# Two heads side by side, on the two halves of the array's columns, in a decoder step's prompt attention

## The chip, the cores and the metric
The kernel runs on one core of one Trainium2 chip. The metric is the device time of one execution in microseconds: 1531.83 us is the median of three runs (1531.2 to 1532.99).

## The reference
One inference step of a two-layer decoder (model width 1024) for a prompt of 512 tokens and eight sample sequences of one token each, all in float32. Layer 0 has a dilated sliding-window softmax attention with 8 heads of 64 (called A here) beside a gated linear attention with 4 heads. Layer 1 (called C) has 16 query heads on 4 key heads; an indexer picks 128 keys for each query, and only these take part. Each layer ends with a SwiGLU FFN and a gated per-layer input. For a query block, attention is

```python
s = jnp.einsum('btngd,btknd->btkng', qg, kg).reshape(bx, t, k, h).astype(jnp.float32) + bias
s = jnp.where(valid[..., None], s, -jnp.inf)
lse = jax.nn.logsumexp(s, axis=2)
p = jnp.exp(s - lse[:, :, None, :]).reshape(bx, t, k, n_kv, grp)
o = jnp.einsum('btkng,btknd->btngd', p.astype(vg.dtype), vg).reshape(bx, t, h, d)
```

The kernel computes C with a mask over all earlier keys in place of a gather, and A with the dilations folded into the bias table.

## The kernel before
Activations lie with features on the 128 partitions and the 520 tokens (512 of the prompt, 8 samples) along the free axis. Every weight matrix is a stream of blocks of 128x1024. SyncE loads a block, ScalarE rounds it (`w_hi`, L1396), POOL takes the rest (`w_lo`, L516), and TensorE multiplies three times (hi by hi, hi by lo, lo by hi; `block_products`, L750). TensorE's queue is one written order: input projection, prompt attention, output projection, FFN, gate, for layer 0 and then layer 1. Engines wait for each other by counting semaphores.

Prompt attention (`attention` on each engine) is a list of units. A unit is a pair `p` of heads, one head `par` of the pair, and a query block `qb` of 128 queries; it covers 128 x (qb + 1) keys. There are 4 pairs in A (32 units) and 8 in C (64 units), and the order is pair, head, query block. A unit goes through these steps:
- `scores` (TensorE, L848 and L851): in C a matmul adds the mask, then two matmuls with the high and low parts of the queries, into one of two score banks.
- `add_bias` (VectorE, L1921): adds the bias from PSUM and takes the maximum.
- `exps` (ScalarE, L1483), then `scale` (VectorE, L1927 and L1929): exponentials and their sum, then division by it.
- `turn` (TensorE, L860): a transpose for each key block. `copy` (ScalarE, L1490) brings the result back into one of two buffers `pt`.
- `out` (TensorE, L872): for each key block a matmul with values as weights. Values of a head are padded with zeros to 128 columns (`vA`, `vC`), so both heads of a pair add into the same bank: 128 partitions, of which the head's own 64 get values and the others zeros.

TensorE's iteration i does scores of unit i, the transposes of unit i-3, the output of unit i-4, and then what `sample_a` or `sample_c` puts in at that i: the samples' attention (L1159 and L1171 in A, whose weights have 64 columns; L1314 and L1331 in C), norms and transposes. When a pair's eight units are done, ScalarE (L1494) and VectorE (L1934) split its result for the output projection.

Before a stage starts, heads are staged: POOL makes high, repeated and low parts of a query head (L612 and L618 in A, `place_q_part` at L700 to L704 in C), ScalarE and VectorE do the same for keys (L1684 and L2162 in A; L1833 and L2306 in C), and POOL zeroes the padding and places the values. In C, VectorE first finds the 128 largest index scores of each query (L2287 and L2291) and makes the masks (L2312).

In the first layer `values_by_token` (L1002) is a group of matmuls whose weights have 64 columns and which go in turns to partitions 0 to 63 and 64 to 127 of one bank; `sample_updates` (L1077) has eight records on one half and then eight on the other.

## Time and profile before

| what | value |
|---|---|
| median of three runs | 1531.83 us (1531.2 to 1532.99) |
| the profiled execution's own time | 1531.57 us |
| its span in the profile | 1529.8 us |
| mean granted TensorE clock | 0.991 |
| TensorE busy | 1496.5 us, 98% |
| VectorE, ScalarE, POOL busy | 623.9, 652.2, 761.6 us |
| first scores of attention A, of attention C | at 199.59 us, at 922.80 us |
| first output-projection matmul after C | at 1038.96 us |

The engines are named PE (TensorE matmuls), PEld (its weight loads), DVE (VectorE), ACT (ScalarE), POOL and SP (SyncE). "L872" is line 872 of the kernel. A float32 matmul leaves two records in the trace, so counts of records are twice the counts of such matmuls in the code. Matmul records overlap: the step from one start to the next tells the rate, and the duration of one does not. Instructions of one kind that follow each other are merged in the timeline, with their count and the time from the first start to the last end.

### The profile page before, as it was taken

Reading aid. Unit: us, or ns where it says so; the run is one execution under the profiler, and the core shown is the slowest. Engines: PE = TensorE matmul, PEld = TensorE weight load, DVE = VectorE, ACT = ScalarE, POOL = GpSimd, SP = SyncE. Lnnn points to the kernel's source line nnn. Section 1 sums busy time; section 2 is a strip of 40 time slices with the busy share of each in tenths; the row PEclk is TensorE's granted clock in tenths of the full one; section 3 lists DMA queues with packets and bytes.
Section 4 is the critical chain, followed back from the end, with each engine's and each line's share of the span. In section 5 each row is a group of like instructions: output and inputs, shape, how many; then the busy total and the mean of one; then the engine's idle time right before and its main releaser. Section 6 shows DMA issues by size and latency. Waiting matters only on the chain.

```text
span 1529.8 us, 30921 instructions
## 1 busy us (share of the span) xinstructions
PE 1496.5 (98%) x12032; PEld 1428.4 (93%) x12032; DVE 623.9 (41%) x1176; ACT 652.2 (43%) x1095; POOL 761.6 (50%) x589
## 2 busy tenths in 40 slices
PE   7999998999999999999999997999999999999998
PEld 6999976699999999999999786999999999999998
DVE  4035556335333333212361796873433233222224
ACT  5242555325344344222464556663443444432234
POOL 4655674064554554555436476324454554554543
PEclk9999989999999999999999998999999999999999
DMA  5321433223233223333234231132222232223332
GB/s 175 91 98 57 152 135 107 70 96 98 83 95 96 84 95 96 97 96 100 93 94 122 90 94 63 54 86 70 83 96 89 92 94 91 89 95 99 107 96 98
DMA packets 52980, 145.84 MB, mean 95 GB/s; under 512 B 5501, under 2 KB 18329, under 8 KB 52394
## 3 DMA queue, kind: packets, MB, share of 16 engines
q1 hardware_dynamic: 50490, 136.12, 28.4%
q10 hardware_dynamic: 2416, 8.72, 1.6%
q8 instruction: 48, 0.79, 0.2%
q14 instruction: 26, 0.21, 0.0%
HBM read 138.06 MB, written 6.76 MB: 95 GB/s over the span
## 4 chain that ended last, share of the span: by engine, by line
PE 91%; DVE 4%; ACT 2%; issue 1%; DMA 1%; POOL 1%; SPq 0%; ACTq 0%; DVEq 0%; POOLq 0%
PE PS L750 74%; PE PS L872 3%; PE PS L965 2%; PE PS L851 2%; PE PS L860 1%; PE PS L788 1%; PE PS L1159 1%; PE PS L1171 1%; DMA w_raw<-in_w 1%; PE PS L1244 1%; PE PS L848 1%; PE PS L1314 1%; DVE act_lo L1901 0%; DVE sqsum L1892 0%; PE PS L1331 0%
## 5 line engine op out<-in xcount | busy, mean ns | idle before, releaser
L516 POOL TENSOR_TENSOR w_lo<-w_raw,w_hi 128x512 fp32r<-128x512 f32 x428 | 594.4, 1409 | 688.1 <-ACT w_hi L1396 680.6
L750 PE MATMUL PS<-act_hi,w_hi 128*128 128x260 f32 x2464 | 701.6, 285 | 0.8 <-DVE act_lo L2178 0.7
L750 PE MATMUL PS<-act_lo,w_hi 128*128 128x260 f32 x2464 | 695.4, 282 | 0.0
L750 PE MATMUL PS<-act_hi,w_lo 128*128 128x260 f32 x2464 | 694.9, 282 | 0.0
L1396 ACT ACTIVATE w_hi<-w_raw 128x1024 fp32r<-128x1024 f32 x214 | 226.9, 1060 | 685.5 <-PE PS L750 665.9
L750 PEld LDWEIGHTS PS<-act_hi,w_hi 128*128 128x128 f32 x2464 | 463.5, 188 | 15.0 <-issue 12.3
L750 PEld LDWEIGHTS PS<-act_lo,w_hi 128*128 128x128 f32 x2464 | 463.8, 188 | 0.4
L750 PEld LDWEIGHTS PS<-act_hi,w_lo 128*128 128x128 f32 x2464 | 464.0, 188 | 0.0
L750 PE MATMUL PS<-h_hi,w_lo 128*128 128x260 f32 x704 | 198.8, 282 | 0.0
L750 PE MATMUL PS<-h_hi,w_hi 128*128 128x260 f32 x704 | 198.6, 282 | 0.0
L750 PE MATMUL PS<-h_lo,w_hi 128*128 128x260 f32 x704 | 198.5, 282 | 0.0
L750 PEld LDWEIGHTS PS<-h_hi,w_hi 128*128 128x128 f32 x704 | 132.6, 188 | 0.0
L750 PEld LDWEIGHTS PS<-h_lo,w_hi 128*128 128x128 f32 x704 | 132.3, 188 | 0.0
L750 PEld LDWEIGHTS PS<-h_hi,w_lo 128*128 128x128 f32 x704 | 132.2, 188 | 0.0
L1981 DVE TENSOR_TENSOR x<-PS,x 128x520 f32<-128x520 f32 x16 | 11.2, 700 | 178.7 <-PE PS L750 178.7
L1966 DVE TENSOR_TENSOR tmp<-PS,nrs 128x520 f32<-128x520 f32 x44 | 30.8, 699 | 110.9 <-PE PS L750 101.2
L1968 DVE TENSOR_TENSOR tmp<-PS,sq 128x520 f32<-128x520 f32 x44 | 30.8, 699 | 103.7 <-ACT sq L1537 103.7
L1892 DVE TENSOR_TENSOR sqsum<-sqsum,sq 128x520 f32<-128x520 f32 x48 | 63.9, 1332 | 21.2 <-ACT sq L1402 20.4
L1972 DVE TENSOR_TENSOR tmp<-PS,tmp 128x520 f32<-128x520 f32 x44 | 30.8, 700 | 94.5 <-PE PS L750 94.5
L1490 ACT ACTIVATE tmp<-PS 128x128 f32<-128x128 f32 (+1 forms) x96 | 41.4, 431 | 59.2 <-PE PS L860 59.2
L1901 DVE SCALAR_TENSOR_TENSOR act_lo<-x,vecs,act_hi 128x520 fp32r<-128x520 f32 x48 | 48.7, 1031 | 21.8 <-ACT act_hi L1407 21.7
L1976 DVE TENSOR_TENSOR h_lo<-tmp,h_hi 128x520 f32 x44 | 34.9, 794 | 40.2 <-ACT h_hi L1541 40.2
(350 smaller groups left out, 1903.7 us busy)
## 6 DMA issues: line engine op xcount, KB each, us to landing
w_raw<-in_w SPq DMA_DIRECT2D x214, 512.0 KB, 3.5
kcA<-in_cache_k SPq DMA_DIRECT2D x8, 512.0 KB, 4.7
biasC<-scratch_rows SPq DMA_DIRECT2D x12, 256.0 KB
vcA<-in_cache_v SPq DMA_DIRECT2D x4, 512.0 KB, 5.2
kcC<-in_pool_k SPq DMA_DIRECT2D x16, 128.0 KB, 2.6
vcC<-in_pool_v SPq DMA_DIRECT2D x16, 128.0 KB, 2.2
out_y<-x SPq DMA_DIRECT2D x7, 260.0 KB, 4.3
x<-in_xT SPq DMA_DIRECT2D x3, 520.0 KB, 6.7
```

What stands on the lines that cost most here:

```text
L516: ins = pool.tensor_tensor(w_lo[:, s, cols], w_raw[:, s, cols], w_hi[:, s, cols].bitcast(F32), ALU.subtract)
L750: mm = pe.matmul(PS[:, 2 * place + half, 0:HALF], w[:, s, j * P:(j + 1) * P], r[:, c, cols], start=first and n == 0 and i == 0, stop=last ...
L851: mm = pe.matmul(PS[:, score_bank(base, i), 0:W], q_of[part][par][:, p % 2, qb * P:(qb + 1) * P], k[:, k_chunk(p), 0:W], start=part == 0 a ...
L872: mm = pe.matmul(PS[:, 4 + p % 2, qb * P:(qb + 1) * P], v_of(p, par, kb), pt[:, i % 2, kb * P:(kb + 1) * P], start=i % 8 == 0, stop=i % 8 ...
L1396: act.activation(w_hi[:, s, :], w_raw[:, s, :], ACT.Copy).then_inc(S("w_hi"), 1)
L1490: act.activation(pt[:, i % 2, 0:W], PS[:, turned_bank(base, i), 0:W], ACT.Copy).then_inc(S("t_c"), 1)
L1892: dve.tensor_tensor(sqsum[:], sqsum[:], sq[:, m % 2, :], ALU.add).then_inc(S("ssum"), 1)
L1901: dve.scalar_tensor_tensor(act_lo[:, c, :], x[:, c, :], vecs[:, g:g + 1], act_hi[:, c, :].bitcast(F32), ALU.mult, ALU.subtract).then_inc(S ...
L1966: dve.tensor_tensor(halves(tmp[:, 1, :]), slot(0), halves(nrs[:]), ALU.mult).then_inc(S("f_a"), 1)
L1968: dve.tensor_tensor(halves(tmp[:, 1, :]), slot(0), halves(sq[:, 0, :]), ALU.mult).then_inc(S("free_v"), 1)
L1972: dve.tensor_tensor(halves(tmp[:, 0, :]), slot(1), halves(tmp[:, 1, :]), ALU.mult).then_inc(S("free_v"), 1)
L1976: dve.tensor_tensor(h_lo[:, bass.ds(f, 1), :], tmp[:, 0:1, :], h_hi[:, bass.ds(f, 1), :].bitcast(F32), ALU.subtract).then_inc(S("h_lo"), 1)
```

## The change
- Units are ordered pair, query block, head: both heads of a pair side by side.
- `out` does two units at once, on odd iterations (units i-5 and i-4). Its matmuls alternate between the heads. Each has a head's 64 value columns as weights and writes that head's 64 partitions. The padded values, their zeroing and their placing are gone.
- `pt` has four buffers; the two new ones are the ones that held padded values (`rs`), which are also the head norm's, hence the wait for the last norm in `copy`.
- In C the keys of the first and second half of the pairs ("T") are staged apart: the first before the stage, the second at iterations 14, 15 (ScalarE) and 18, 19 (VectorE). The third mask is made after the first unit's bias. The head norm before the last moves behind the first exponentials. Query staging starts a block earlier.
- The samples' queries in C are placed by two copies for each half of the heads, in place of two for each pair.
- POOL's long element-wise instructions are done in two halves.
- Bias rows of a later pair are asked for when the last unit of the same head two pairs before has its bias added.

```diff
-        pt = tmp[:, :, 0:SEQ]
+        pt = (tmp[:, 0, 0:SEQ], tmp[:, 1, 0:SEQ], rs[:, 0, 0:SEQ], rs[:, 1, 0:SEQ])
...
         def units_of(pairs):
 
-            return [(p, par, qb) for p in range(pairs) for par in range(2) for qb in range(QB)]
+            return [(p, par, qb) for p in range(pairs) for qb in range(QB) for par in range(2)]
...
             def bias_a(p, par):
 
-                sp.wait_ge(S("t_x"), BASE_A + 8 * (p - 2) + 4 * par + 6)
+                sp.wait_ge(S("t_x"), BASE_A + 8 * (p - 2) + par + 9)
...
+            def in_halves(out, t, u, op):
+
+                n = out.shape[-1] // 2
+                for half in range(2):
+                    at = (slice(None),) * (len(out.shape) - 1) + (slice(n * half, n * half + n),)
+                    ins = pool.tensor_tensor(out[at], t[at], u[at], op)
+                return ins
+
             def low(b, s):
 
                 pool.wait_ge(S("w_hi"), b + 1)
-                for half in range(2):
-                    cols = slice(DM // 2 * half, DM // 2 * half + DM // 2)
-                    ins = pool.tensor_tensor(w_lo[:, s, cols], w_raw[:, s, cols], w_hi[:, s, cols].bitcast(F32),
-                                             ALU.subtract)
-                ins.then_inc(S("w_lo"), 1)
+                in_halves(w_lo[:, s, :], w_raw[:, s, :], w_hi[:, s, :].bitcast(F32),
+                          ALU.subtract).then_inc(S("w_lo"), 1)
...
-            def zero_v(par):
-                pool.memset(vA[par][:, :, :, other[par]], 0.0).then_inc(S("A_zero"), 1)
...
-            def place_v(pair, par):
...
             def first_q_c(n):
-                if n == 14:
+                if n == 13:
                     pool.wait_ge(S("i_r"), 24)
                     pool.wait_ge(S("d_z"), 3)
-                    pool.memset(vC[0][:, :, :, other[0]], 0.0).then_inc(S("C_zero"), 1)
-                if 14 <= n < 18:
+                if 13 <= n < 17:
                     pool.wait_ge(S("hn_ok"), n + 2)
-                    for k in ((0, 1), (2,), (3, 4), (5,))[n - 14]:
+                    for k in ((0, 1), (2,), (3, 4), (5,))[n - 13]:
                         place_q_part(0, k)
 
             products_in(1, first_q_c)
 
-            pool.wait_ge(S("hn_ok"), 19 + 2)
-            pool.memset(vC[1][:, :, :, other[1]], 0.0).then_inc(S("C_zero"), 1)
-            pool.wait_ge(S("C_zero"), 2)
             for p in range(1, PAIRS_C):
...
                 def out(i):
-                    p, par, qb = units[i]
-                    if par == 0 and qb == 0:
+                    p, _, qb = units[i]
+                    if qb == 0:
                         pe.wait_ge(S("t_o"), base // 8 + p + 1)
-                    pe.wait_ge(S("t_c"), base + i + 3)
-                    if qb == 0 and valued is not None:
-                        valued(p, par)
+                    if p == 0:
+                        valued(qb)
+                    pe.wait_ge(S("t_c"), base + i + 4)
                     for kb in range(qb + 1):
-                        mm = pe.matmul(PS[:, 4 + p % 2, qb * P:(qb + 1) * P], v_of(p, par, kb),
-                                       pt[:, i % 2, kb * P:(kb + 1) * P], start=i % 8 == 0,
-                                       stop=i % 8 == 7 and kb == qb)
-                    mm.then_inc(S("t_v"), 1)
+                        for par in range(2):
+                            mm = pe.matmul(PS[HD * par:HD * par + HD, 4 + p % 2, qb * P:(qb + 1) * P], v_of(p, par, kb),
+                                           pt[(i + par) % 4][:, kb * P:(kb + 1) * P], start=qb == 0,
+                                           stop=qb == QB - 1 and kb == qb)
+                    mm.then_inc(S("t_v"), 2)
...
-                        out(i - 4)
+                    if i >= 5 and i % 2:
+                        out(i - 5)
...
-            def values_staged_a(p, par):
-                if p == 0 and par == 0:
-                    pe.wait_ge(S("hn_ln"), 8 + 1)
-                pe.wait_ge(S("A_zero"), par + 1)
-                pe.wait_ge(S("A_st"), 4 * p + 3 + par)
+            def values_staged_a(qb):
+                pe.wait_ge(S("hn_ln"), 8 + 1)
+                pe.wait_ge(S("A_v"), qb + 1)
...
                 def copy(i):
                     W = P * (units[i][2] + 1)
                     act.wait_ge(S("t_t"), base + i + 3)
-                    act.wait_ge(S("t_v"), base + i + 1)
-                    act.activation(pt[:, i % 2, 0:W], PS[:, turned_bank(base, i), 0:W], ACT.Copy).then_inc(S("t_c"), 1)
+                    act.wait_ge(S("t_v"), base + (max(i - 2, 0) // 2) * 2)
+                    if i == 2:
+                        act.wait_ge(S("hn_ok"), (19 if base else 8) + 2)
+                    act.activation(pt[i % 4][:, 0:W], PS[:, turned_bank(base, i), 0:W], ACT.Copy).then_inc(S("t_c"), 1)
...
-                    if q is not None:
+                    if q is not None and not (final and l == 1):
...
-            def sample_q(t):
-                act.wait_ge(S("hn_ok"), 11 + t + 1 + 2)
+            def sample_q(T):
+                act.wait_ge(S("hn_ok"), 11 + 4 * T + 4 + 2)
                 for r in range(2):
                     rows = slice(HD * r, HD * r + HD)
-                    cols = qzC[rows, t // 4 * NS:(t // 4 + 1) * NS, :].rearrange("p b c -> p (b c)")
-                    c0 = 64 * r + NS * t
-                    act.activation(cols[:, c0:c0 + 7 * 129 + 1:129], yC[rows, 10 + t, SEQ:NT],
+                    by_token = qzC_flat[rows, NS * P * T:NS * P * T + NS * (P + 1)].rearrange("p (b c) -> p b c", c=P + 1)
+                    c0 = 64 * r + 4 * NS * T
+                    act.activation(by_token[:, :, c0:c0 + 3 * NS + 1:NS],
+                                   yC[rows, 10 + 4 * T:14 + 4 * T, SEQ:NT].rearrange("p t b -> p b t"),
                                    ACT.Copy).then_inc(S("C_st8"), 1)
 
-            def values_c(par):
+            def values_c():
 
                 for n in range(2):
                     act.wait_ge(S("v_vt"), n + 5)
-                    by_head = PS[:, 6 + n, :].rearrange("p (k t d) -> p t k d", k=2, t=2)
-                    act.activation(vC[par][:, :, 2 * n:2 * n + 2, HD * par:HD * par + HD],
-                                   by_head[:, :, :, HD * par:HD * par + HD], ACT.Copy).then_inc(S("C_st8"), 1)
+                    act.activation(vtokC[:, :, 2 * n * P:(2 * n + 2) * P].rearrange("p t (k d) -> p t k d", d=P),
+                                   PS[:, 6 + n, :].rearrange("p (k t d) -> p t k d", k=2, t=2),
+                                   ACT.Copy).then_inc(S("C_st8"), 1)
 
             def first_staging_c(n):
 
                 if n == C_BLOCKS - 1:
-                    values_c(0)
-                    act.wait_ge(S("act_free"), 4 + KC - 1 + 2)
-                    for k, rows in ((act_hi, slice(0, HD)), (act_lo, slice(HD, P))):
-                        act.activation(k[rows, 3:8:4, 0:SEQ], yC[rows, 6:8, 0:SEQ], ACT.Copy).then_inc(S("k_hi"), 1)
+                    act.wait_ge(S("act_free"), 4 + KC - 1 + 1)
+                    high_keys(0, 0)
+                    high_keys(1, 0)
+                    values_c()
+
+            def high_keys(par, T):
+                rows = slice(HD * par, HD * par + HD)
+                act.activation((act_hi, act_lo)[par][rows, 3 + 4 * T, 0:SEQ], yC[rows, 6 + T, 0:SEQ],
+                               ACT.Copy).then_inc(S("k_hi"), 1)
 
             last_head_rms_c, last_high_c = products_in(1, indexer, first_staging_c)
             def sample_c(i):
 
-                if i == 3:
+                if i == 0:
+                    last_head_rms_c(1)
+                elif i == 3:
                     last_head_rms_c()
                 elif i == 4:
                     last_high_c()
-                elif i == 5:
-                    act.wait_ge(S("hn_ok"), 19 + 2)
-                    values_c(1)
                 elif i in (6, 7):
...
+                elif i in (14, 15):
+                    if i == 14:
+                        act.wait_ge(S("act_free"), 4 + KC - 1 + 2)
+                    high_keys(i - 14, 1)
...
-            def low_keys(par):
+            def low_keys(par, T):
                 k = (act_hi, act_lo)[par]
                 rows, others = slice(HD * par, HD * par + HD), slice(HD - HD * par, P - HD * par)
-                dve.wait_ge(S("k_hi"), 3 + par)
-                dve.tensor_tensor(k[others, 3:8:4, 0:SEQ], yC[rows, 6:8, 0:SEQ], k[rows, 3:8:4, 0:SEQ].bitcast(F32),
-                                  ALU.subtract).then_inc(S("k_split"), 1)
-
-            low_keys(0)
-            for qb in range(1, QB):
+                dve.wait_ge(S("k_hi"), 3 + 2 * T + par)
+                dve.tensor_tensor(k[others, 3 + 4 * T, 0:SEQ], yC[rows, 6 + T, 0:SEQ],
+                                  k[rows, 3 + 4 * T, 0:SEQ].bitcast(F32), ALU.subtract).then_inc(S("k_split"), 1)
+
+            def mask(qb):
                 W = P * (qb + 1)
                 dve.tensor_scalar(maskC[:, qb, 0:W], work[qb][:, 0:W], GONE, NEG, ALU.not_equal,
                                   ALU.mult).then_inc(S("topk"), 1)
-            low_keys(1)
-            dve.wait_ge(S("topk"), QB)
+
+            low_keys(0, 0)
+            mask(1)
+            low_keys(1, 0)
+            mask(2)
+            dve.wait_ge(S("topk"), QB - 1)
...
-                if i == 6:
+                if i == 0:
+                    mask(3)
+                    dve.wait_ge(S("topk"), QB)
+                elif i in (18, 19):
+                    low_keys(i - 18, 1)
```

## Rows read from the trace of the kernel before

**Rows 1.** The page, part 1: busy us (share of the span) xinstructions.
```profile
PE 1496.5 (98%) x12032; PEld 1428.4 (93%) x12032; DVE 623.9 (41%) x1176; ACT 652.2 (43%) x1095; POOL 761.6 (50%) x589
```

**Rows 2.** The page, part 4: chain that ended last, by engine.
```profile
PE 91%; DVE 4%; ACT 2%; issue 1%; DMA 1%; POOL 1%; SPq 0%; ACTq 0%; DVEq 0%; POOLq 0%
```

**Rows 3.** Groups by line, L872: count | busy us, mean ns | idle before.
```profile
L872 PE MATMUL PS<-tmp,rs 128*128 128x128 f32 x240 | 35.4, 278 | 0.7 <-ACT tmp L1490 0.7
...
L872 PE MATMUL PS<-tmp,vtokC 128*128 128x128 f32 x160 | 23.6, 278 | 2.0 <-issue 1.6 <-ACT tmp L1490 0.2
...
L872 PE MATMUL PS<-tmp,vstA 128*128 128x128 f32 x80 | 12.7, 292 | 0.1
```

**Rows 4.** Timeline of PE, attention C: start us, us, what, [idle before].
```profile
967.51 0.33 PE L851 MATMUL PS<-act_lo,q_hiC 128*128 128x128 f32 x1
...
969.92 0.60 PE L860 MATMUL PS<-const,pC 128*128 128x128 f32 x4
...
970.94 0.48 PE L848 MATMUL PS<-maskC,identR 128*128 128x512 f32 x1
971.26 0.40 PE L851 MATMUL PS<-act_lo,q_hiC 128*128 128x512 f32 x1
...
971.84 1.06 PE L872 MATMUL PS<-tmp,vtokC 128*128 128x128 f32 x8
...
972.65 0.31 PE L851 MATMUL PS<-act_hi,q_hiC 128*128 128x128 f32 x1
```

**Rows 5.** Windows: stretch, length, busy us (count) by engine, PEclk, DMA, GB/s.
```profile
975.00:1000.00 25.00, 24.81 (x197) 22.96 (x196) 22.11 (x78) 17.33 (x54) 11.81 (x15) 1.00 0.18 57
1000.00:1035.00 35.00, 34.13 (x270) 31.91 (x270) 25.14 (x95) 22.58 (x68) 5.79 (x7) 1.00 0.27 81
920.00:930.00 10.00, 5.42 (x29) 4.60 (x28) 8.43 (x12) 5.18 (x10) 6.54 (x5) 0.80 0.01 2
```

**Rows 6.** Timeline of PE around L1002, column halves in turns.
```profile
88.52 0.28 PE L750 MATMUL PS<-act_hi,w_lo 128*128 128x260 f32 x1
88.73 1.97 PE L1002 MATMUL PS<-const,yA 128*64 128x128 f32 x32
90.63 0.39 PE L750 MATMUL PS<-act_hi,w_hi 128*128 128x260 f32 x1
90.86 0.28 PE L750 MATMUL PS<-act_lo,w_hi 128*128 128x260 f32 x1
```

**Rows 7.** Timeline of PE, L1077: eight on one half, then eight.
```profile
166.29 1.58 PE L1077 MATMUL PS<-vt,kz 8*64 8x128 f32 x16
```

**Rows 8.** Timeline of PE, attention A: L872 ahead of 64-column L1159.
```profile
237.13 0.39 PE L872 MATMUL PS<-tmp,vstA 128*128 128x128 f32 x2
...
237.45 1.95 PE L1159 MATMUL PS<-kcA,yA 128*64 128x257 f32 x8
```

**Rows 9.** Timeline at the entry of attention C: VectorE, then PE.
```profile
920.83 1.76 DVE L2306 TENSOR_TENSOR act_hi<-yC,act_hi 64x1024 fp32r<-64x1024 f32 x1 [1.61 <-ACT act_hi L1833]
...
925.59 2.19 DVE L2306 TENSOR_TENSOR act_lo<-yC,act_lo 64x1024 fp32r<-64x1024 f32 x1
...
927.81 0.29 DVE L1921 CUSTOM_DVE_ANT_0 xC<-PS,biasC 128x128 f32<-128x128 f32 x1
...
922.93 0.27 PE L851 MATMUL PS<-act_hi,q_loC 128*128 128x128 f32 x1
```

**Rows 10.** Timeline, later in that entry: PE, then POOL.
```profile
928.21 0.66 PE L848 MATMUL PS<-maskC,identR 128*128 128x384 f32 x1 [3.61 <-issue]
...
942.84 0.92 PE L1309 MATMUL PS<-sbC 33*128 33x257 f32 x2 [1.53 <-ACT qzC L1816]
...
941.58 1.26 POOL L704 TENSOR_TENSOR q_loC<-yC,q_hiC 64x512 fp32r<-64x512 f32 x1
```

**Rows 11.** Timeline at the entry of attention A: PE, then POOL.
```profile
200.65 0.37 PE L851 MATMUL PS<-act_hi,q_hiA 128*128 128x256 f32 x1
...
201.44 1.27 POOL L618 TENSOR_TENSOR act_lo<-yA,act_hi 64x512 fp32r<-64x512 f32 x1
```

More of the change, by code:

```diff
@@ L682, in _ @@
                     split_q(pair, par)
-                    pool.wait_ge(S("A_st"), 4 * pair + par + 1)
-                for par in range(2):
-                    place_v(pair, par)
+                    pool.wait_ge(S("A_st"), 2 * pair + par + 1)
                 if pair == 1:
@@ L703, in place_q_part @@
                 else:
-                    pool.tensor_tensor(qC[1][par][own[par], p % 2, :], q, high.bitcast(F32),
-                                       ALU.subtract).then_inc(S("C_st"), 1)
+                    in_halves(qC[1][par][own[par], p % 2, :], q, high.bitcast(F32),
+                              ALU.subtract).then_inc(S("C_st"), 1)
                 pool.wait_ge(S("C_st"), 6 * p + k + 1)
@@ L832, in products_in, with attention @@
                 return lambda: head_sum(q, None)
-            def attention(pairs, base, ps, q_of, k_chunk, v_of, staged, between=None, masked=False, valued=None):
+            def attention(pairs, base, ps, q_of, k_chunk, v_of, staged, valued, between=None, masked=False):
                 units = units_of(pairs)
@@ L1470, in products_in @@
                 b = b0 + last + 2
-                return lambda: head_rms(q, q % 2), lambda: high(b, b % 2)
+                return lambda back=0: head_rms(q - back, (q - back) % 2), lambda: high(b, b % 2)
             def attention(pairs, base, xs, ps, stat, between=None):
@@ L1784, in indexer @@
                     act.wait_ge(S("hn_ok"), 11 + 2)
-                    for b in range(4):
-                        act.activation(kcC[:, b, :, PAST], yC[:, 6:8, SEQ + b], ACT.Copy).then_inc(S("C_st8"), 1)
-                if n >= 15:
-                    sample_q(n - 15)
+                    act.activation(kcC[:, :, :, PAST], yC[:, 6:8, SEQ:SEQ + 4].rearrange("p t b -> p b t"),
+                                   ACT.Copy).then_inc(S("C_st8"), 1)
                 if 13 <= n < 17:
@@ L2243, in _ @@
             then(dve.memset(iwz[:], 0.0))
-            then(dve.memset(qzC[:], 0.0))
+            then(dve.memset(qzC, 0.0))
             dve.wait_ge(S("y_rs"), 17 + 5)
```

73 lines of the change are left out of this document (27 added, 46 removed).

## The prediction
> **What bounds the kernel now.** I read the page first. TensorE is busy for 98% of the span [rows 1], and the chain of waits is TensorE for 91% of it [rows 2]. So a change pays if it shortens TensorE's queue in a stage, or a wait that TensorE has there. The projections and the FFN keep their matmuls. What can move is attention A (units 0 to 31, from about 200 to 298 us) and attention C (units 0 to 63, from about 923 to 1039 us).
>
> Next come the groups by line. The products of probabilities and values (L872) are 480 records, two for each of 240 matmuls [rows 3]. The timeline shows how densely they run. Between 967.51 and 972.65 us TensorE does four units with no gap, 5.14 us [rows 4]. The x8 entry there lasts 1.06 us, and one record 0.278 on average [rows 3], so a start follows the last by (1.06 - 0.28)/7 = 0.112 us.
>
> Last come the busy times by stretch [rows 5]. In the middle of attention C TensorE has no idle time worth the name, VectorE is busy 22.11 of 25 us (18 units, 1.23 us each) and ScalarE 17.33. TensorE is the bound, with VectorE close behind it. At the entry of C TensorE waits instead: 5.42 of 10 us busy at a mean granted clock of 0.80, VectorE 8.43.
>
> **The change part by part.**
>
> *Column halves in turns.* The count of L872 records stays 480; each now loads 64 columns of weights, writes 64 partitions, and alternates between the halves of the array. The trace of before has that very form at L1002: values by token, weights 128x64, 128 moving columns, halves in turns. 32 records last 1.97 us, and with 0.28 for one again, (1.97 - 0.28)/31 = 0.0545 us from start to start [rows 6]. In L1002 the moving operand is the same for both halves; here each head has its own. I take 0.055: 480 x (0.112 - 0.055) = 27.4 us less. Bounds: 0.055 below; above, 0.087 from L1077, eight records on one half and then eight on the other ((1.58 - 0.28)/15) [rows 7], or 0.112, no gain.
>
> *Entering and leaving that form.* L1002 stands between matmuls of the plain form. From the start at 88.52 plus one normal step of 0.12 (88.64) to the second plain start, 90.86, less a step (90.74), are 2.10 us for 32 records [rows 6]. 32 x 0.055 is 1.76, so going in and out costs 0.34 us. Counted alike, ten plain records (L860 x4, L872 x6) have nothing on top: from 969.92 to 971.26 less 0.21, the 512 columns of the matmul between at 2.4 GHz, are 1.13 us, 0.113 each [rows 4]. A second place agrees on the way in: L872 x2 at 237.13 should end its turn at 237.35, and L1159 (64 columns too) starts at 237.45, 0.10 later [rows 8]; leaving takes the other 0.24. The change has 4 groups for each of 12 pairs: 48 x 0.34 = 16.3 us more. By size, at 0.057 a record: the group of query block 0 (4 records) loses 0.11 us, those of blocks 1, 2 and 3 (8, 12, 16 records) win 0.12, 0.34 and 0.57. That is 0.92 us a pair, 11.1 in all.
>
> The Trainium skill bears on this: "TensorEngine Tiling (Array Packing)", Key Properties, says that changing the tiling mode, not just the tile, drains TensorE, which speaks against a change that switches 96 times. The trace agrees, with the 0.34 us above for both switches. The same page's Theoretical Speedup gives up to 2x where the stationary side has 64 columns or fewer; with that and no drain, L872 alone would give back about 27 us.
>
> *Groups that meet 64-column sample work.* In A seven of the new groups (iterations 5, 9, 11, 15, 23, 27, 31) stand right before L1159 or L1171, which pay their own 0.34 now. They share one stay in the form: 7 x 0.34 = 2.4 us less. TensorE's queue is shorter by 13.5 us.
>
> *What is late next.* VectorE. In 975 to 1000 us a pair costs TensorE 8 x 25/18 = 11.1 us and VectorE 9.8 [rows 5]; TensorE falls to 10.2. Two score banks and three buffers do not smooth all of it: widths now come as 128, 128, 256, 256, 384, 384, 512, 512, an output group waits for both heads' copies, and on iterations without one only scores and transposes cover ScalarE's copy of up to 512 columns. I charge 0.35 us a pair, 4.2 in all (bounds 0 and the whole 0.92 a pair). Steady part: 9.3 us less.
>
> *Entry of C.* Now VectorE idles 1.61 us for ScalarE's copy of the keys (1024 columns) until 920.83, does 1.76 us of them, then three masks until 925.6 and 2.19 us of the other head, and adds the first bias at 927.81, though the scores were there at 923.2 [rows 9]. After: ScalarE copies 64x512 for each head before the values and waits for chunk 3 alone, so the keys are there as the searches end (920.83 - 1.61 = 919.2); VectorE does keys half as wide (0.9 + 1.1 us) and two of the three masks (two thirds of the 3.0 us between the rows, 2.0 at most), and the third after the first bias. 919.2 + 4.0 = 923.2, just when the scores come: 4.6 us earlier. From there the old stage also has a half-clock stretch after its 3.61 us stall, (the 384-wide mask matmul took 0.66 us), and beside unit 8 a wait of 1.53 us for ScalarE's ten small copies of sample queries [rows 10]; the change makes four of them all. Against that, unit 9 is the other head, and needs all six staging steps of pair 1 from POOL, the last of which ended at 942.84 [rows 10], not the first three. They start once the last norm is through, and that too comes some 5 us earlier. I take 6 us less (bounds 3 and 9).
>
> *Entry of A.* Unit 1 is now head 1. Its q halves leave POOL at 202.71, while unit 1 ran at 200.65 [rows 11]. TensorE waits about 2 us there, less what it waited anyway for VectorE's copies in the next steps. I take 1.5 us more (bounds 0 and 3). POOL loses its zeroing and placing of values; they are not on the path after the entry.
>
> *Tails.* The last output group of a layer has 16 records of both heads behind the last copy: 16 x 0.055 + 0.2 = 1.1 us where 8 x 0.112 = 0.9 stood, and two 512-wide units precede it instead of 384 and 512. 0.4 us a layer, 0.8 in all (0 to 2).
>
> *Cost nothing:* POOL's instructions in halves (one more instruction each; POOL is busy half of the span [rows 1], and runs ahead of TensorE; if that cover were gone, some 90 extra starts at an estimated 0.1 us or less would cost 9 us). Bias rows are asked for up to three units later but eight units ahead of use. The copies' wait on output products is covered by four buffers; the third buffer waits for the last norm, which ScalarE waits for at the iteration before in A.
>
> **Sum.** -9.3 (steady) - 6 (entry C) + 1.5 (entry A) + 0.8 (tails) = -13.0. I round to -12.5 for small mishaps. The profiled execution took 1531.57 us (span 1529.8), 0.26 below the median 1531.83, so 1519.1, and I write 1519.
>
> **Rivals.**
> - *The halves do not overlap here* (two different moving streams, both accumulating into one bank). Then 480 records at 0.112 win nothing, the switches cost 16.3 - 2.4, the entries and tails give back 3.7: +10.2, 1542 us. The point from which it is slower: 480 x (0.112 - r) + 2.4 + 3.7 = 16.3, so from r = 0.091 us a record. For it: L1077 at 0.087 on one half at a time. Against: L1002 at 0.055, same bank and width. Chance 0.07.
> - *VectorE becomes the bound*: the steady part gives only the shared stays, 2.4, and the entries do theirs: -6.1, 1525.5; with less from the entry of C, 1529. For it: VectorE at 88% in 975 to 1000. Against: only 72% in 1000 to 1035 [rows 5]. Chance 0.20, of which 0.06 within the bound of no change.
> - *Everything lands*: no stalls, entry of C at 9: -13.5 - 9 + 0.8 = -21.7, 1510. Without any cost of switching it would be -27.4 - 3.7, 1500.5, against which stand the 0.34 us of [rows 6]; chance 0.01. (That is what the Theoretical Speedup of the Trainium skill's page "TensorEngine Tiling (Array Packing)" would give.) Together 0.10 for below 1513.
> - The forecast, 1513 to 1525: 0.63.
>
> **How the numbers follow.** No change is within 0.2%, 3 us, about what a measurement can tell. Faster: 0.63 + 0.10 + 0.14 = 0.87; same 0.06; slower 0.07 (the first rival). The range leaves out the slow rival and the lowest end: 1511 to 1528.
>
> **What would show it.** L872 as 128*64 with starts 0.055 us apart inside a group; a four-unit stretch of C without sample work down from 5.14 to about 4.7 us; the first bias of C near 923 and its unit 9 near 937; attention A shorter by 4 to 5 us and C by 9 to 10. Wrong would be: 0.11 between starts, VectorE at 95% with TensorE idling behind it, or the projections, which should not change, moving by more than 1 us.

## The result, and the profile after

| | before | after |
|---|---|---|
| median of 7 runs, us | 1531.83 (1531.2 to 1533.82) | 1524.95 (1522.11 to 1528.1) |
| profiled execution: own time, span, us | 1531.57, 1529.8 | 1527.53, 1525.7 |
| attention A: first norm sum to the first projection matmul behind it | 198.63 to 297.36: 98.73 | 199.74 to 298.61: 98.87 |
| the stages between | 624.23 | 624.37 |
| attention C, counted alike | 921.59 to 1038.96: 117.37 | 922.98 to 1035.24: 112.26 |
| from there to the end of the span | 490.84 | 490.46 |

The ratio is 0.9957, interval 0.9944 to 0.9971: some 6.6 us faster, where 12.5 were forecast. The profiled execution after lies 2.6 us above the median, so the stages of the two profiles differ by 4.1 us in all and not by 6.6. The stages that should not move stay within 0.4 us (A starts 1.1 us later; in the twelve runs below it starts between 198.65 and 199.85). C gives 5.1 us, A nothing.

By stretches of C: up to the fourth pair's first scores 45.13 us where 51.06 stood, the fourth to seventh pair 49.06 for 49.92, and from the eighth pair to the end of the stage 18.07 for 16.39. The end of C became longer.

The page of the kernel after, part 1, as [rows 1], and then busy times by stretch, as [rows 5]:

```profile
PE 1486.5 (97%) x12032; PEld 1401.5 (92%) x12032; DVE 608.3 (40%) x1178; ACT 651.3 (43%) x1080; POOL 774.9 (51%) x668
...
975.00:1000.00 25.00, 23.95 (x204) 19.28 (x202) 18.77 (x72) 17.59 (x53) 11.15 (x16) 1.00 0.24 68
1000.00:1035.00 35.00, 32.35 (x265) 25.59 (x266) 23.61 (x91) 23.10 (x66) 5.55 (x8) 0.95 0.20 67
920.00:930.00 10.00, 8.02 (x55) 7.15 (x53) 8.98 (x27) 8.02 (x21) 7.16 (x9) 1.00 0.03 10
```

TensorE's busy time fell by 10.0 us and the span by 4.1. In the middle of C it was busy 24.81 of 25 us and is now 23.95, while VectorE fell from 22.11 to 19.28 (77%): TensorE now idles for 1.05 us there, though VectorE has more room than before. At the entry of C it is busy 8.02 of 10 us instead of 5.42.

The outputs (L872 before, L847 now) in the timeline of PE in C, then the groups by line with their forms, as [rows 3, 4]:

```profile
980.79 0.27 PE L825 MATMUL PS<-act_lo,q_loC 128*128 128x128 f32 x1
981.52 0.66 PE L834 MATMUL PS<-const,pC 128*128 128x128 f32 x4 [0.45 <-DVE pC L1908]
982.10 0.88 PE L847 MATMUL PS<-tmp,vtokC 128*64 128x128 f32 x12
982.91 0.38 PE L822 MATMUL PS<-maskC,identR 128*128 128x256 f32 x1
...
L847 PE MATMUL PS<-rs,vtokC 128*64 128x128 f32 x192 | 14.8, 291 | 1.6 <-ACT rs L1463 1.4
L847 PE MATMUL PS<-tmp,vtokC 128*64 128x128 f32 x128 | 10.8, 290 | 1.4 <-ACT tmp L1463 1.3
```

Twelve records last 0.88 us, so (0.88 - 0.28)/11 = 0.055 us from start to start, as forecast. Ahead of them stands something new, a wait for VectorE's division of probabilities (0.45 us). The waits of PE by what they wait for, A and then C (us in total, times, longest):

```profile
PE PS L1144 <- issue: 2.4, 1, 2.4
PE PS L1132 <- DMA kcA<-in_cache_k: 2.2, 1, 2.2
PE PS L825 <- POOL act_lo L510: 2.1, 1, 2.1
...
PE PS L822 <- DVE statC L1900: 3.7, 5, 1.6
PE PS L847 <- ACT rs L1463: 1.4, 4, 0.7
PE PS L847 <- ACT tmp L1463: 1.3, 2, 1.1
```

The longest one in C (1.57 us at 957.73) is not VectorE's own slowness. Its timeline, and then SP's:

```profile
952.33 0.55 DVE L1908 TENSOR_SCALAR pC<-pC,statC 128x512 f32<-128x512 f32 x1
957.38 0.29 DVE L1900 CUSTOM_DVE_ANT_0 sq<-PS,biasC 128x128 f32<-128x128 f32 x1 [4.50 <-DMA biasC<-scratch_rows]
...
939.44 9.98 SPq L466 DMA_DIRECT2D kcC<-in_pool_k  x8
949.46 4.11 SPq L343 DMA_DIRECT2D biasC<-scratch_rows  x3
```

Unit 17 is now pair 2's second head (it was unit 20). Its bias stands on SP behind eight key pages that wait for sample scores, is issued at 949.46 and there at 957.38; VectorE idles 4.50 us.

### The profile page after: what moved, and what is told of

Read it like the earlier page. It is cut to its first block, busy times and chain, and to the rows that moved or that the text cites. A ratio compares the mean times of both kernels' runs of the same rounds, so it can differ in the third digit from the quotient of the medians.

```text
span 1525.7 us, 30982 instructions
## 1 busy us (share of the span) xinstructions
PE 1486.5 (97%) x12032; PEld 1401.5 (92%) x12032; DVE 608.3 (40%) x1178; ACT 651.3 (43%) x1080; POOL 774.9 (51%) x668
## 4 chain that ended last, share of the span: by engine, by line
PE 90%; DVE 3%; ACT 2%; DMA 2%; issue 1%; POOL 1%; SPq 0%; ACTq 0%; DVEq 0%; POOLq 0%
PE PS L724 75%; PE PS L940 2%; PE PS L847 2%; PE PS L825 2%; PE PS L762 1%; PE PS L834 1%; PE PS L1144 1%; PE PS L1132 1%; PE PS L1217 1%; DVE act_lo L1880 1%; DMA vcC<-in_pool_v 1%; DMA biasC<-scratch_rows 1%; PE PS L822 1%; DMA kcA<-in_cache_k 0%; DVE sqsum L1871 0%
## 5 line engine op out<-in xcount | busy, mean ns | idle before, releaser
L724 PEld LDWEIGHTS PS<-act_hi,w_hi 128*128 128x128 f32 x2464 | 463.5, 188 | 15.2 <-issue 12.7
L1960 DVE TENSOR_TENSOR x<-PS,x 128x520 f32<-128x520 f32 x16 | 11.2, 699 | 178.7 <-PE PS L724 178.7
L1514 ACT ACTIVATE h_hi<-tmp 128x520 f32 (+1 forms) x44 | 28.1, 640 | 26.8 <-DVE tmp L1953 26.8
```

The source lines that it names most:

```text
L724: mm = pe.matmul(PS[:, 2 * place + half, 0:HALF], w[:, s, j * P:(j + 1) * P], r[:, c, cols], start=first and n == 0 and i == 0, stop=last ...
```

## The experiments

Twelve kernels, numbered 1 to 4 and 6 to 13, each timed beside the kernel before, and the ratio is to that. Stage times are from one profile each, read as in the table above, so a stage can move by some us with the granted clock of that one execution (see run 10).

| run | median us | ratio, interval | A | C |
|---|---|---|---|---|
| 1 full-width outputs | 1532.15 | 1.0000, 0.9991 to 1.0008 | 101.20 | 116.92 |
| 2 one half first | 1529.49 | 0.9969, 0.9957 to 0.9982 | 100.17 | 113.48 |
| 3 early bias | 1523.22 | 0.9937, 0.9924 to 0.9950 | 98.43 | 109.09 |
| 4 GpSimd whole | 1528.06 | 0.9966, 0.9954 to 0.9978 | 99.21 | 113.16 |
| 6 = 3 + blocks 0, 3, 1, 2 | 1516.96 | 0.9910, 0.9896 to 0.9924 | 94.89 | 105.47 |
| 7 = 3 + both waits of A | 1512.93 | 0.9882, 0.9868 to 0.9897 | 86.13 | 108.78 |
| 8 = 6 + both waits of A | 1515.15 | 0.9881, 0.9865 to 0.9896 | 94.07 | 109.19 |
| 9 = 3 + short divisions | 1520.26 | 0.9926, 0.9913 to 0.9939 | 97.53 | 108.74 |
| 10 = 7 + blocks 0, 3, 1, 2 in C | 1511.54 | 0.9860, 0.9845 to 0.9875 | 90.36 | 106.46 |
| 11 = 3 + keys later | 1517.89 | 0.9897, 0.9882 to 0.9912 | 95.92 | 108.88 |
| 12 = 3 + logarithm earlier | 1520.63 | 0.9912, 0.9898 to 0.9926 | 94.60 | 110.27 |
| 13 = 9 + light GpSimd | 1521.40 | 0.9923, 0.9909 to 0.9937 | 99.45 | 107.41 |

Pairs are compared by the distance from one pair's first scores to the next pair's. For the second to seventh pair of C: before 19.32, 12.90, 11.60, 11.63, 12.90, 13.79; after 16.20, 16.99, 11.68, 11.97, 12.11, 13.30.

**1. Full-width outputs**

```diff
-    PS[HD*par:HD*par+HD, ...], values of one head (64 columns), start=qb == 0
+    PS[:, ...], values of both heads (128 columns), start=qb == 0 and par == 0
```

> The changed kernel, but each product of probabilities and values loads 128 value columns (both heads of the pair) and writes all 128 partitions, so nothing of it is in column halves; heads are summed together, so the output is not the attention's. Order of units, entries and everything else are those of the changed kernel (1524.95 us; attention A 98.87 us, C 112.26 us from the first unit's stage start to the first matmul behind it). Theory as predicted (halves save 0.057 us a record, each stay in the form costs 0.34 us, some of it already paid by sample work): TensorE's queue gets 13.5 us longer, less up to 4 us that VectorE's waits took: 1534 to 1538 us, A +3 to +5, C +6 to +8. Rival, VectorE is the bound in the steady part: under 3 us more in all, 1525 to 1528. Rival, the switching is dearer than read and the halves bring nothing: 1525 or less.

Measured: 6.6 us slower than the change by the ratios (1.0000 against 0.9957), A +2.3, C +4.7; between the theory's range and its rival's. In the steady part the term shows unmixed: the fourth to sixth pair take 12.97, 12.94 and 13.14 us, against 11.91, 11.98 and 12.12 with halves (run 3), 1.01 us a pair where the prediction's groups add to 0.92. In the stage it is less, because the third pair, where the bias was late anyway, is shorter than after (14.60 against 16.99). (The seventh pair gives less, 0.52: 13.79 against 13.27.) The second thing that it shows is the larger: TensorE has the same kinds and numbers of records there as the kernel before, and takes 12.97 and 12.94 us for the fourth and fifth pair where that took 11.60 and 11.63. The new order, with its outputs two units at a time, costs 1.3 us in each of these two. In the sixth and seventh pair it costs 0.2 and nothing (13.14 and 13.79 against 12.90 and 13.79). What differs is the work beside the units: in the profile of the kernel after, the sample products (L1302) are 56 records and 6.8 us in the sixth and seventh pair together, and 8 records and 1.0 us in the fourth and fifth.

**2. One half first, then the other**

```diff
-    for kb in range(qb + 1):
-        for par in range(2):
+    for par in range(2):
+        for kb in range(qb + 1):
```

> The changed kernel, but inside a group all records of the first head's half of the columns come before those of the second head's. Theory: two records overlap only when they lie on different halves, so without turns each takes 0.087 to 0.112 us and not 0.055: 480 x 0.032 to 0.057 = 15 to 27 us more, less what VectorE's waits hide (up to 5): 1535 to 1552 us. Rival, a 64-column record is short in any order: 1525, x16 groups still 1.09 us.

Timeline of PE in C, the four group sizes:

```profile
998.18 1.58 PE L847 MATMUL PS<-rs,vtokC 128*64 128x128 f32 x16
1002.16 0.44 PE L847 MATMUL PS<-tmp,vtokC 128*64 128x128 f32 x4
1004.78 0.66 PE L847 MATMUL PS<-rs,vtokC 128*64 128x128 f32 x8
1007.68 1.14 PE L847 MATMUL PS<-tmp,vtokC 128*64 128x128 f32 x12
```

In turns they last 0.44, 0.66, 0.88 and 1.09 us. So with two or four records on one half before the other, nothing is lost; with six, 0.26 us, and with eight, 0.49 ((1.58 - 0.28)/15 = 0.087 a step, as in [rows 7]). That is 0.75 us a pair and 9 in all, not 15 or more, and the fourth to sixth pair of C show it: 12.44, 12.73 and 12.88 us, 0.68 more than in run 3. The whole is only 1.8 us slower than the change (0.9969 against 0.9957, overlapping), for the late bias hides some here too (third pair 14.68), and the second and third pair of A last 46.18 us against 46.02, though their groups are slower too. The theory holds for long runs on one half alone, and its price was too high.

**3. The bias asked for earlier**

```diff
     for b in range(4, NS):
         sp.wait_ge(S("s_ks"), NS + b - 3)
         key_pages(b)
-    bias_c(2, 1)
+        if b == 4:
+            bias_c(2, 1)
```

> The changed kernel, but the bias of pair 2's second head in attention C is asked for behind the key pages of sample token 4, not behind those of token 7. Theory: the 4.50 us that VectorE idled for this transfer until 957.38 (unit 17) and the 1.57 us wait and half-clock stretch of TensorE behind it go: attention C 109 to 110 us instead of 112.26, the whole 1521.5 to 1523. Rival, VectorE would have idled anyway and a later wait takes its place: C 112, the whole 1524 to 1525.5. Rival, the key pages now come late for the sample scores at units 14 to 17: a wait for them of 1 us or more, 1525 or more.

C 109.09 instead of 112.26, as in the theory; the whole at 0.9937 instead of 0.9957, 3.1 us less, with a median 0.2 above the theory's range. No wait for the bias is left in VectorE's list for C; the third pair takes 13.07 us instead of 16.99, the second 17.69 instead of 16.20. The second rival holds in part: a wait of 1.4 us for key pages appears, which the gain pays for. All later runs contain this edit.

**4. GpSimd's instructions whole again**

```diff
-    for half in range(2): ins = pool.tensor_tensor(out[half], t[half], u[half], op)
+    ins = pool.tensor_tensor(out, t, u, op)
```

> The changed kernel, but every GpSimd operation that the change cut into two halves is one instruction again (the low parts of the weights stay in halves, as before the change). Theory as predicted (the halves cost nothing and bring nothing): 1524.5 to 1525.5 us. Rival, a long GpSimd instruction holds up VectorE or ScalarE beside it (the port that they share), and the halves shorten this: 1527 or more. Rival, the extra starts cost time on the path at the two entries: 1522 to 1524.

0.9966 against 0.9957, A +0.3, C +0.9: the sign of the first rival, within the intervals. The longest division of VectorE in C is 1.49 us here, 0.88 with halves, and PE's waits for divisions (pC) are 2.4 us in C instead of 0.5. The fourth and fifth pair take 12.93 and 12.50 us, against 11.91 and 11.98 in run 3, with VectorE busy for 10.89 and 10.65 us against 9.89 and 9.75 and ScalarE unchanged (8.98 and 9.01 against 8.93 and 8.91). So the halves bring 1.5 us in these two pairs, and the late bias hides it in the stage (third pair 14.41 against 16.99). "Cost nothing" was right as a sum and "bring nothing" was not; the two kernels' intervals overlap, so what they bring to the whole stays open.

**6. The wide units apart**

```diff
-    for qb in range(QB)
+    for qb in ((0, 3, 1, 2) if p else range(QB))
```

> The changed kernel with the early bias of the third run, and with the query blocks of every pair but a layer's first in the order 0, 3, 1, 2, so that the two 512-wide units of a pair are no longer followed by two 128-wide ones. Base: attention A 98.43 us, C 109.09 us, 11.91 and 11.98 us for the fourth and fifth pair of C, where TensorE's queue should be 10.7. Theory: 1.2 us a pair are waits at the pair's boundary, where the scale, exponentials and copies of 512 columns have only 128-wide scores and transposes beside them; a more even order halves them: fourth and fifth pair 11.2 to 11.5, C 105 to 107, whole 1519 to 1521 us. Rival, the lost time is inside the groups or the switches, wherever they stand: pairs 11.9, 1523. Rival, a worse pattern: the widths 128 then 512 starve TensorE at another place: pairs above 12.2, 1525 or more.

The fourth pair takes 10.86 us (below the 11.2 forecast), the fifth 11.22, instead of 11.91 and 11.98, and C 105.47; the whole, 1516.96, is lower than the theory had it. The two pairs in run 3 and then in run 6 (length, then busy PE, PEld, DVE, ACT, POOL):

```profile
963.84:975.75 11.91, 10.97 (x88) 8.13 (x87) 9.89 (x37) 8.93 (x29) 5.70 (x9) 1.00 0.13 43
975.75:987.73 11.98, 11.24 (x94) 8.62 (x92) 9.75 (x38) 8.91 (x29) 5.56 (x9) 1.00 0.13 46
...
960.90:971.76 10.86, 10.41 (x88) 8.00 (x87) 9.98 (x39) 8.53 (x28) 5.39 (x9) 1.00 0.13 45
971.76:982.98 11.22, 10.93 (x95) 8.58 (x93) 9.92 (x38) 9.17 (x28) 5.24 (x9) 1.00 0.13 49
```

Only the order of the widths differs, so most of the extra time of run 1 comes from where wide and narrow units meet, and not from the records or the switches of form. Idle time of TensorE accounts for half of it (0.94 and 0.74 us in run 3, 0.45 and 0.29 in run 6); the other half lies within its busy time, where the profile does not divide it. In the sixth and seventh pair, with the sample products beside them, the order moves only 0.1 and 0.2 us (12.00 and 13.10 against 12.11 and 13.27). (The 94.89 us of A are not evidence: see run 10.)

**9. VectorE's divisions on 128 columns**

```diff
-    dve.tensor_scalar(ps[i % 3][:, 0:W], ...)
+    dve.tensor_scalar(ps[i % 3][:, 0:P], ...)
```

> The changed kernel with the early bias, and VectorE divides only the first 128 columns of each unit's probabilities by their sum (the others stay undivided, so the output is not the attention's); the same instructions, signals and TensorE work. It takes some 0.3 us a unit off VectorE. Theory, VectorE's chain at the pair's boundary holds TensorE: fourth and fifth pair of C from 11.9 to 11.0 or less, C below 104, whole 1514 to 1518 us. Rival, ScalarE's exponentials and copies hold it: 11.6 to 11.9, C 107 to 109, whole 1521 to 1523. Rival, TensorE's own queue is that long (the switches are dearer than 0.34 us): no change, with waits no smaller.

12.28 and 11.74 us for the fourth and fifth pair: no change, and the theory seemed to have fallen. But the timeline of VectorE at the boundary, and GpSimd's beside it, show that the edit hardly took anything away:

```profile
964.73 0.76 DVE L1909 TENSOR_SCALAR pC<-pC,statC 128x128 f32<-128x128 f32 x1
966.12 0.73 DVE L1909 TENSOR_SCALAR sq<-sq,statC 128x128 f32<-128x128 f32 x1
...
964.68 1.41 POOL L511 TENSOR_TENSOR q_loC<-yC,q_hiC 64x256 fp32r<-64x256 f32 x2
```

A division of 128 columns lasts 0.73 or 0.76 us beside GpSimd's staging of the next pair's queries, and 0.285 where GpSimd is idle; VectorE's busy time a pair fell only from 9.83 to 9.59.

**13. And GpSimd's staging of pairs 3 to 7 on 16 columns**

```diff
-    q = yC[own[par], 10 + p, 0:SEQ]
+    n = SEQ if p < 3 else 16
+    q = yC[own[par], 10 + p, 0:n]
```

> The changed kernel with the early bias, VectorE dividing only the first 128 columns of each unit's probabilities, and GpSimd staging only the first 16 columns of the queries of pairs 3 to 7 of C (both leave part of the attention uncomputed). The ninth run did not test VectorE: its 128-wide divisions still took 0.65 to 0.78 us beside GpSimd's instructions, where 0.28 is the least. Theory, these held divisions at the pair's boundary are what TensorE waits for: the divisions drop to 0.3 us, VectorE falls to 8.5 us or less a pair, and the fourth and fifth pair of C go from 11.9 to 11.2 or less. Rival, the chain through ScalarE (exponential and copy of 512 columns, one behind the other, beside 128-wide work of TensorE) holds it: 11.6 to 12.0 for both pairs. Rival, the switching of forms: 11.9 and no wait smaller.

Divisions by tile in that stretch, run 13, and windows of the fourth and fifth pair (length, then busy PE, PEld, DVE, ACT, POOL):

```profile
L1910 DVE TENSOR_SCALAR pC<-pC,statC x11: 285/286/288, 966.9 to 987.8; 128x128 f32<-128x128 f32 x11
...
966.28:977.82 11.54, 10.40 (x88) 8.04 (x86) 8.30 (x37) 8.87 (x30) 1.49 (x10) 1.00 0.13 43
977.82:988.96 11.14, 10.84 (x94) 8.51 (x92) 7.92 (x37) 8.63 (x28) 1.49 (x10) 1.00 0.13 47
```

Divisions at 0.286 us and 11.54 and 11.14 us a pair, 0.6 less than 11.91 and 11.98 on average. That lies between the theory (11.2 or less) and its rival (11.6 to 12.0). So what GpSimd's instructions take from VectorE is about half of the 1.2 us; the rest remains with VectorE busy for 8.1 us a pair, which leaves ScalarE's chain or the order itself; no run separates these. The whole is no clearly faster than run 3 (0.9923, 0.9937): C was 1.7 us shorter in its profile, and A and what stands ahead of it 1.0 us longer each. In the fourth and fifth pair of the kernel before, divisions lasted up to 1.11 us beside GpSimd, and TensorE was busy 23.04 of 23.23 us. The contention is old, the lack of cover new. The Trainium skill, "SBUF — State Buffer", Who interferes with whom, says that a VectorE instruction in one of its two-port modes, which `tensor_scalar` can take, contends with GpSimd: whoever issues first has the shared port pair for the whole instruction, and the other blocks fully. The trace agrees: 0.285 us alone against 0.76, and the longest division falls from 1.49 to 0.88 us with GpSimd's instructions in halves.

**7, 11, 12. The waits of A**

```diff
-    SCORES_A = (5, 6, 8, 9, 11, 12, 14, 15)
+    SCORES_A = (5, 6, 8, 9, 11, 12, 15, 16)          # 7 and 11
-    if i in (8, 11, 15, 19, 21): rms_b(...)
+    if i in (8, 11, 15, 19, 20): rms_b(...)          # 7 and 12
```

> The changed kernel with the early bias in C, and in A two waits taken away: the sample scores of tokens 6 and 7 one iteration later (15 and 16), so that the keys have time to land, and ScalarE's last gated-norm logarithm one iteration earlier (20), so that the sample values at iteration 22 find it done. Theory: TensorE's waits for the key DMA (2.2 us) and for the logarithm (1.6 to 2.4 us) go, with some half-clock time behind them: attention A 94 to 96 us instead of 98.4 to 98.9, whole 1519 to 1521 us. Rival, VectorE is late there anyway and the waits only change their names: A 97.5 to 99, whole 1522.5 to 1524.

> The changed kernel with the early bias and, in A, only the sample scores of tokens 6 and 7 one iteration later. The seventh run took 12.3 us off A for 3.8 us of waits taken away. Theory, a wait costs twice, once itself and once by the half clock behind it, and each of the two waits of A has its own share: A 91 to 94 us, whole 1517 to 1519. Rival, the key wait alone does it: A 86 to 89, whole 1512 to 1514. Rival, it does nothing alone, since the next wait at the sample values is longer then: A 97 to 99, whole 1522 to 1523.5.

> The changed kernel with the early bias and, in A, only ScalarE's last gated-norm logarithm one iteration earlier. Theory of two shares: A 91 to 95 us, whole 1516 to 1519, the key wait of 2.2 us still there. Rival, the logarithm alone does it: A 86 to 89, whole 1512 to 1514. Rival, nothing alone: A 97 to 99, whole 1522 to 1523.5.

The second and third pair of A together, in windows (length, PE busy, and behind POOL the granted clock): the kernel after, run 11, run 12, run 10 (which has both edits). The kernel after has A's instructions as run 3 has them, which 7, 11 and 12 are built on.

```profile
226.39:250.34 23.95, 21.80 (x130) 13.57 (x129) 12.07 (x38) 13.78 (x40) 11.25 (x15) 1.00 0.58 156
250.34:272.41 22.07, 16.92 (x94) 9.21 (x93) 14.85 (x44) 11.11 (x35) 11.61 (x15) 0.85 0.18 65
```

```profile
225.96:245.60 19.64, 19.64 (x122) 12.52 (x120) 11.80 (x37) 13.10 (x39) 11.25 (x15) 1.00 0.56 157
245.60:268.22 22.62, 18.81 (x102) 10.53 (x101) 14.51 (x44) 11.96 (x36) 10.98 (x15) 0.85 0.31 93
```

```profile
226.50:250.58 24.08, 21.81 (x131) 13.58 (x129) 11.86 (x38) 13.79 (x40) 11.43 (x15) 1.00 0.56 156
250.58:268.23 17.65, 14.47 (x93) 8.43 (x92) 14.78 (x44) 11.27 (x35) 11.63 (x15) 1.00 0.24 83
```

```profile
225.59:245.22 19.63, 19.63 (x122) 12.50 (x121) 11.82 (x37) 13.09 (x39) 11.24 (x15) 1.00 0.55 158
245.22:263.08 17.86, 15.96 (x101) 9.51 (x100) 14.41 (x44) 11.96 (x36) 10.98 (x15) 1.00 0.40 116
```

46.02, 42.26, 41.73 and 37.49 us: the keys are worth 3.8, the logarithm 4.3, both 8.5, for waits of 2.2 and 2.4 us. In run 3's own profile these two pairs took 48.03 us, with granted clocks of 0.93 and 0.77, so each share is known to some 2 us only. The two shares add, as the theory of runs 11 and 12 had it. The whole is 1517.89 us in run 11, inside its range, and 1520.63 in run 12, 1.6 above it; A is 95.92, 1.9 above its range, and 94.60, inside it. The half clock behind a wait is seen at the logarithm: in the kernel after the granted clock is 0.50 from 264 to 268 us, behind that wait, and with the logarithm in time the third pair runs at 1.00 instead of 0.85. The second pair was at 1.00 in any case; there one sample-score group (1.96 us) moved on into the third, whose idle time took most of it (22.62 us in run 11, 22.07 after). In run 12 the key wait is still there, 2.3 us. Run 7, with both, gained more than its theory said: A 12.7 us below the kernel after, of which 8.2 in these two pairs (37.83 us) and 4.5 in the first pair, which no edit touched (against run 3: 12.3, of which 10.2 and 1.2). Run 10 shows that this first pair varies by itself.

**8 and 10. All together**

> All of it together: early bias, the two waits of A, and the order 0, 3, 1, 2 of query blocks. Theory: the gains add, A 93 to 95.5, C 105 to 107, whole 1515 to 1518 us. Rival: neither adds, 1522 to 1524.

> The changed kernel with the early bias, the two waits of A taken away (as in the seventh run), and the query blocks in the order 0, 3, 1, 2 in attention C alone. Theory: the parts add where each was seen in a profile, A 86 to 88 us (seventh run 86.13), C 105 to 106 (sixth run 105.47): whole 1508 to 1511 us. Rival, the 94.07 us of A in the eighth run came from the earlier stages and not from the order in A, and half-clock stretches return: A 92 or more, whole 1513 to 1516.

```diff
-    for qb in range(QB)
+    for qb in ((0, 3, 1, 2) if p and pairs == PAIRS_C else range(QB))      # 10; in 8 for both layers
```

Run 8 is where its theory had it, 1515.15 us, but no faster than 7; its profile was the slowest of its four runs (1520.13 us, clock 0.987), so its stage times say little (C 109.19, above the theory's 105 to 107). Run 10 has the lowest median, 1511.54 us, 0.5 above its theory's range, 21 us below the kernel before at 0.9860; its interval overlaps that of run 7. Its A of 90.36 is above the theory and below the rival, its C of 106.46 0.5 above the theory, and no half-clock stretch returned in the second and third pair (37.49 us). The first pair is what differs: 25.25 us against 20.71 in run 7. The windows of PE over it, run 7 and run 10 (length, PE busy, clock, DMA share, GB/s):

```profile
206.00:210.00 4.00, 4.00 (x36) 1.00 0.01 2
210.00:215.00 5.00, 5.00 (x28) 0.80 0.65 266
```

```profile
206.00:210.00 4.00, 4.00 (x27) 0.78 0.00 0
210.00:215.00 5.00, 5.00 (x28) 0.62 0.39 160
```

The instructions of A are the same in both, and behind the same 2.1 us wait (until 203.7) they are granted 1.00 or 0.78; what decides between the two, no run shows. In the thirteen profiles with the new order the first pair lasts 20.7 to 22.0 us three times (3, 6, 7) and 23.9 to 25.3 us otherwise.

## Why the prediction was right, and where it was too high

The time fell into the range and the sign was right; of the 12.5 us, 6.6 came. The range was wide enough for several terms that went wrong in the same direction: that it held was in part luck, though both the step of the records and the entry of C came as forecast. By stretches, the terms add to 7.7 us for C up to its fourth pair (6 + 3 x 0.57), 2.3 for the fourth to seventh and 0.2 for the rest of C; measured were 5.9 and 0.9 less, and then 1.7 more instead of less. For A they add to 2.8, and nothing came.

- *Halves in turns, 0.055 us a record*: right, 0.055. *Going in and out of the form costs 0.34 us*: in run 3 the three transposes before an x8 group end their turn at 974.74 + 3 x 0.11 = 975.07, and the next plain start is 975.75. The step from that one to the next is some 0.04 us longer than usual, which is counted in:

```profile
974.74 0.49 PE L835 MATMUL PS<-const,pC 128*128 128x128 f32 x3
975.16 0.66 PE L848 MATMUL PS<-rs,vtokC 128*64 128x128 f32 x8
975.75 0.33 PE L826 MATMUL PS<-act_hi,q_hiC 128*128 128x128 f32 x1
```

  0.72 - 8 x 0.055 = 0.28 us. Net, the fourth to sixth pair show 1.01 us a pair (run 1 against 3) and the seventh 0.52; 0.92 was forecast.
- *Overlap needs turns* (the bound of 0.087): true for six and more records on one half, not for four (run 2).
- *Stalls of 0.35 us a pair*: **the step that failed.** Run 3 takes 11.95 us for the fourth and fifth pair where the queue is 11.6 - 1.0 = 10.6, so it is 1.3 there, above the bound of 0.92 that I gave. I had put it down to VectorE's load, 88% before; that fell to 77%. What limits is how the widths meet (run 6: 0.9 us less with the wide units apart). That the 128-wide work behind two 512-wide units covers neither the division nor the copy is the reading that fits this and run 13, which puts half of it down to GpSimd; the step of the chain that holds the other half is not shown. In the sixth and seventh pair, where sample products give cover, the forecast held: they gain 0.8 and 0.5 us, 0.57 was forecast. The four together gain 0.9 us (49.92 to 49.06) and not 2.3. The rival "VectorE becomes the bound" has nearly the right time, 1525.5, with the wrong cause: TensorE idles while VectorE is at 77%.
- *Entry of C, 6 us*: right. The first bias is added 1.39 us into the stage (was 6.22): 4.8 earlier, 4.6 forecast. Here is VectorE's row, as [rows 9]:

```profile
920.64 0.96 DVE L2285 TENSOR_TENSOR act_hi<-yC,act_hi 64x512 fp32r<-64x512 f32 x1
922.39 1.12 DVE L2285 TENSOR_TENSOR act_lo<-yC,act_lo 64x512 fp32r<-64x512 f32 x1
924.37 0.29 DVE L1900 CUSTOM_DVE_ANT_0 xC<-PS,biasC 128x128 f32<-128x128 f32 x1
```

  The third pair starts 28.14 us in, where it was 38.16: 10.0 less, and the next distance gives 4.1 of it back.
- *Tails, 0.4 us a layer*: too low for C. From the eighth pair's first scores to the end of the stage it takes 18.07 us where it took 16.39: 1.7 more, where 0.4 more, less 0.57 for the pair, was forecast. In run 3, with nothing changed there, it is 17.10. The same instruction behind the same wait, in the kernel after and in run 3:

```profile
1027.60 0.77 PE L822 MATMUL PS<-maskC,identR 128*128 128x512 f32 x1 [1.24 <-DVE statC L1900]
...
1023.53 0.51 PE L823 MATMUL PS<-maskC,identR 128*128 128x512 f32 x1 [1.25 <-DVE statC L1901]
```

  Some 1.0 us is thus the clock of that one execution (granted 0.77 from 1025 to 1030 us, where run 3 has 1.00 throughout), and 0.7 us stays at the full clock, with waits for VectorE and for the last copy. In A the last stretch is 1.1 us shorter (26.20 for 27.31).
- *"Bias rows are asked for up to three units later but eight units ahead of use"*: **failed** for one row of twelve. I counted the units of its wait and not what SP has in front of it. The transfer is issued 3.4 us before VectorE is free for it (949.46 against 957.38 - 4.50) and takes 7.9 us. Worth 3.2 us (run 3).
- *Entry of A, 1.5 us*: right in kind, 2.1 us of wait for GpSimd's low part; the second pair starts 26.65 us into the stage, 0.6 later than before (26.01). The clock behind the wait moves the first pair by 4.5 us between profiles (run 10).
- *Attention A shorter by 4 to 5 us*: failed, and not even the sum of my terms for A (4 x 0.57 + 2.4 - 1.5 - 0.4 = 2.8). Run 1 shows that the halves do give 2.3. Two waits took it back. Key 6 is loaded once key 4 is used (237.60); the units became shorter, so three of them no longer cover the transfer: 2.2 us, where 0.5 stood (0.7 in run 1, whose units are longer). And the sample values at iteration 22 need ScalarE's logarithm, queued behind the exponentials of unit 21: 2.4 us. The kernel before waited for ScalarE too, 2.2 us at L1124, which is 1.1 now (L1099); with the entry's 2.1 us, TensorE's waits in A add to 10.4 us where they were 5.4. A faster engine met what had been just in time.
- *GpSimd's halves cost nothing*: right as a sum (run 4). An extra start is dearer than my 0.1 us: two instructions of 64x256 take 1.41 us where one of 64x512 took 1.26, 0.15 more, which GpSimd's slack covers.

## What to carry to other kernels

Where TensorE is the bound with 99% of its time used, count for each reordering how much work of TensorE stands beside each unit's chain on the other engines, and not the load of these engines: the order of the widths alone moved 0.9 us a pair in two pairs with nothing else beside the units, and 0.1 and 0.2 us in two that had sample products beside them. A request's distance is that of everything in front of it on its queue. A wait of 2 us was worth some 4 in these profiles, so the small waits that a gain uncovers deserve a look before the gain is written off: taking away three of them and changing the order of the widths made 6.6 us into 21.

## What the hardware showed that I had not expected

- Waits of 2.2 and 2.4 us in A are worth 3.8 and 4.3 us by one profile each; behind the second the granted clock is 0.85 over a pair, and 1.00 without it.
- Four 64-column records on one half and then four on the other take no longer than eight in turns (0.66 us); eight and eight take 1.58 against 1.09 (run 2).
- The same instructions get 0.78 or 1.00 of the clock behind the same wait, and the first pair of A lasts 25.3 or 20.7 us. A kernel's times spread by as much, and with the clock: the four of run 7 are 1510.21, 1512.55, 1513.31 and 1515.31 at clocks 0.997, 0.996, 0.996 and 0.994. In which stretch each of them lost it is not shown, as only one was profiled.
- A VectorE division of 128 columns takes 0.285 us alone and up to 0.79 beside GpSimd's halves (run 9), and halving GpSimd's instructions lowers the longest division in C from 1.49 to 0.88 us.
